# Sending tokens to their experts and back by products with a 0/1 matrix instead of through DRAM

## The chip, the cores and the metric

The kernel runs on one core of one Trainium2 chip. The metric is the device time of one execution in microseconds. Before the change it is 827.94 us, the median of three runs (826.21 to 828.65). The profile is of one more execution, and TensorE is PE in it, VectorE DVE, ScalarE ACT, GpSimd POOL, SyncE SP.

## The reference

One layer of a decoder for 256 prompt tokens and 8 sample tokens, all in fp32 with a width of 1024. Two attention mixers (a sparse one with 64 or 256 kept keys, and a stick-breaking one) are mixed by gates and projected; then comes a mixture of experts. Only its end is touched here:

```python
h = x + mixed @ w_out                      # 264 tokens x 1024
t = rmsnorm(h) * ln2_g
g  = top 1 of 4 groups (softmax of t @ w_rg + b);  e1, e2 = top 2 of the 8 experts in that group
combine[token, expert] = the two normalised expert weights times the group's weight, else 0
for every expert of 32:                    # w_gate, w_up: 1024 x 256, w_down: 256 x 1024
    hid = silu(t @ w_gate[e]) * (t @ w_up[e])
    y  += (hid * combine[:, e]) @ w_down[e]
out = rmsnorm(h + y) * ln_f_g
```

The three weight matrices of an expert are 1 MB each, 96 MB in all (100.66 million bytes), and all of them are read.

## The kernel before

Tokens are held in three tiles of rows (128, 128 and 8 tokens, `TILES`). Each expert has room for `CAP` = 32 tokens, and four experts form a quad of 128 slots. There are eight quads (`NQ`), and up to four more (`NQX` = 12), in branches, for tokens over 32 of one expert.

Routing. VectorE chooses experts from the router's logits (L1789 to L1821) and, from a rank that TensorE counts, gives each token two row numbers, one for each of its experts (L1830 to L1855): the row of a slot in a table of all slots. GpSimd scatters the tokens' numbers by these addresses to `table_dram` (L566) and loads the table to SBUF (L570). ScalarE has stored the normalised rows in `x2_dram` (L1374). Per quad GpSimd gathers 128 rows of `x2_dram` into `xg` (L577), TensorE transposes them (`turn`, L1099), ScalarE copies them to `xgT` (L1383).

Experts. `two_experts` (L1069) takes a pair of the quad at a time: 16 fp32 matmuls for gate and up (L1076; stationary 128x32 tokens, moving 128x512 weights; each expert writes its own 32 partitions), silu on ScalarE (L1390), the product on VectorE (L1877), two transposes, a copy, 8 matmuls for down (L1094). Every fp32 matmul is two records in the profile. ScalarE copies the result of a quad and stores it in `y_dram` (L1401), whose overflow part SyncE filled with zeros far ahead (L422).

Return. When the last store has landed, GpSimd gathers for each of the three tiles the first and the second expert's row (L592), and VectorE adds them with their weights to the residual `x_rows` (L1891, L1893). Then come the sum of squares (L1416), the mean (L1896), the power on GpSimd (L594), the scaling (L1899) and the stores of the output.

Weights. Four slots in `arena` hold one quad's weights. SyncE's queue is first in, first out, and all weights go through it. The first four experts are loaded ahead, during the output projection. Then, in a loop, gate and up of a pair are refilled when that pair's gate and up product is done (`s_gu`, L482), and down when its down product is done (`s_down`, L485). The order of work on each engine is written out by hand, and every engine takes its instructions in order. Ahead of all this SyncE waits at L436 for GpSimd's memset of `zero_i` (L557), which stands behind GpSimd's last gather of the attention caches, and only then issues w_proj_a and w_proj_b (L455, L456), for which TensorE waits at L1012.

## Time and profile before

| | |
|---|---|
| median of three runs | 827.94 us |
| the profiled execution's own time | 832.18 us |
| its span, first to last instruction | 830.3 us |
| busy: PE, PEld, DVE, ACT, POOL | 629.7, 356.3, 314.2, 149.9, 129.1 us |
| moved by DMA | 245.12 MB, mean 295 GB/s |
| mean granted TensorE clock | 0.864 |

The span covers all but 1.9 us of the execution's own time. A busy share is an average over stages with different limits; the slices and windows tell which engine is busy in which stage. [...] The DMA share is the mean busy share of 16 DMA engines and can come out a little over 1.

### The profile page before, as it was taken

What the parts mean: (1) busy time and instruction counts of PE and PEld (TensorE: products, weight loads), DVE (VectorE), ACT (ScalarE), POOL (GpSimd) and SP (SyncE); (2) the same over time, 40 slices, a digit from 0 to 9 for tenths busy, and PEclk for the clock granted to TensorE, in tenths of its full rate; (3) what the DMA queues carried; (4) which work ended last, traced back from release to release, by engine and by line L of the source; (5) the groups of instructions that cost most, each with busy time, mean ns of one, the idle gap of its engine ahead of it and who ended that gap; (6) DMA issues with size and microseconds to landing.
All of it is one profiled execution on the core that took longest, in us unless ns stands there. A gap on an engine that the chain in (4) does not pass through costs nothing.

```text
span 830.3 us, 7873 instructions
## 1 busy us (share of the span) xinstructions
PE 629.7 (76%) x3108; PEld 356.3 (43%) x3108; DVE 314.2 (38%) x490; ACT 149.9 (18%) x282; POOL 129.1 (16%) x119
## 2 busy tenths in 40 slices
PE   4969898997997898766899861586777877778710
PEld 3856764676885455325774251121222222222200
DVE  3079998987899870320230155000000000000005
ACT  2124033324104515330000100110110101101101
POOL 2434222111115352111000003100000000000020
PEclk9998899999999796987799955598998899989965
DMA  9997899588657889577789010199999999999631
GB/s 339 413 411 275 313 382 409 198 322 325 242 193 262 318 294 402 204 293 298 273 325 396 34 52 0 52 350 396 399 398 402 400 394 398 400 403 398 261 128 57
DMA packets 123916, 245.12 MB, mean 295 GB/s; under 512 B 14163, under 2 KB 86371, under 8 KB 113612
## 3 DMA queue, kind: packets, MB, share of 16 engines
q1 hardware_dynamic: 103932, 140.33, 46.0%
q0 software_dynamic: 14832, 94.98, 29.7%
q10 hardware_dynamic: 5120, 9.37, 3.1%
q8 instruction: 22, 0.36, 0.2%
q14 instruction: 10, 0.08, 0.0%
HBM read 232.66 MB, written 12.00 MB: 295 GB/s over the span
## 4 chain that ended last, share of the span: by engine, by line
PE 36%; SPq 23%; DVE 16%; DMA 9%; ACT 6%; issue 6%; POOL 2%; ACTq 1%; POOLq 0%; DVEq 0%
SPq L443 19%; PE PS L603 8%; PE PS L1030 5%; SPq L446 4%; DVE arena L1473 4%; PE PS L1021 4%; DVE x_rows L1477 4%; PE PS L1076 4%; PE PS L947 2%; DMA arena<-in_w_proj_b 2%; PE PS L1094 2%; DMA temp<-in_cache_k_a,page_idx 2%; PE PS L724 2%; DMA arena<-in_w_up 1%; PE PS L883 1%
## 5 line engine op out<-in xcount | busy, mean ns | idle before, releaser
L1076 PE MATMUL PS<-arena,temp 128*32 128x512 f32 x512 | 138.1, 701 | 37.4 <-DMA arena<-in_w_up 36.0
L603 PE MATMUL PS<-xT,arena 128*128 128x264 f32 x608 | 142.7, 394 | 4.6 <-ACT arena L1271 4.2
L603 PEld LDWEIGHTS PS<-xT,arena 128*128 128x128 f32 x608 | 116.2, 194 | 26.1 <-ACT arena L1271 4.8
L1877 DVE TENSOR_TENSOR temp<-PS,temp 64x256 f32<-64x256 f32 x16 | 6.8, 422 | 266.5 <-ACT temp L1390 266.5
L1076 PEld LDWEIGHTS PS<-arena,temp 128*32 128x32 f32 x512 | 39.5, 125 | 132.4 <-issue 132.4
L1473 DVE TENSOR_TENSOR arena<-arena,x_rows 128x2048 f32<-128x2048 f32 x32 | 73.0, 2283 | 28.8 <-DMA x_rows<-q_dram 28.7
L1477 DVE TENSOR_REDUCE x_rows<-arena 128x32 f32<-128x2048 f32 x32 | 73.2, 2288 | 1.1
L1094 PE MATMUL PS<-arena,temp 128*32 128x512 f32 x256 | 58.0, 594 | 12.3 <-ACT temp L1394 12.3
L503 POOL DMA_INDIRECT arena<-in_cache_k_b,unit_idx x32 | 39.5, 1234 | 147.5 <-DVE x_rows L1477 142.5
L503 POOL DMA_INDIRECT arena<-in_cache_v_b,unit_idx x32 | 37.6, 1176 | 78.4 <-PE PS L947 57.8
L503 POOL DMA_INDIRECT temp<-x_dram,slot_tok x9 | 8.6, 958 | 225.2 <-PE PS L1103 223.7
L1030 PE MATMUL PS<-temp,xT 128*128 128x512 f32 (+1 forms) x96 | 41.5, 593 | 1.1 <-DVE xT L1760 1.1
L1390 ACT ACTIVATE temp<-PS 64x256 f32<-64x256 f32 x16 | 6.1, 378 | 192.3 <-PE PS L1076 192.3
L1094 PEld LDWEIGHTS PS<-arena,temp 128*32 128x32 f32 x256 | 15.0, 109 | 44.4 <-issue 34.6
L1103 PE MATMUL PS<-consts,temp 128*128 128x128 f32 x72 | 11.2, 303 | 23.7 <-DMA temp<-x_dram,slot_tok 23.7
L1030 PEld LDWEIGHTS PS<-temp,xT 128*128 128x128 f32 (+1 forms) x96 | 14.9, 157 | 27.2 <-issue 27.2
L1138 ACT COPY arena<-PS 128x264 f32<-128x264 f32 x22 | 8.3, 379 | 85.7 <-PE PS L603 85.7
L1103 PEld LDWEIGHTS PS<-consts,temp 128*128 128x128 f32 x72 | 9.3, 197 | 30.5 <-issue 30.5
L1194 ACT COPY temp<-PS 128x512 f32<-128x512 f32 x32 | 17.5, 588 | 24.6 <-PE PS L724 24.6
L1021 PE MATMUL PS<-oaT,arena 128*128 128x264 f32 x64 | 17.5, 421 | 3.0 <-DMA arena<-in_w_proj_b 3.0
L947 PE MATMUL PS<-arena,xT 128*32 128x512 f32 x128 | 18.9, 705 | 0.0
L1767 DVE TENSOR_TENSOR x_rows<-PS,x_rows 128x512 f32<-128x512 f32 (+1 forms) x6 | 4.1, 687 | 38.3 <-PE PS L1030 38.3
(319 smaller groups left out, 722.1 us busy)
## 6 DMA issues: line engine op xcount, KB each, us to landing
arena<-in_w_gate SPq DMA_DIRECT2D x32, 1024.0 KB, 11.6
arena<-in_w_up SPq DMA_DIRECT2D x32, 1024.0 KB, 12.0
arena<-in_w_down SPq DMA_DIRECT2D x32, 1024.0 KB, 11.2
arena<-in_w_in SPq DMA_DIRECT2D x9, 2048.0 KB, 11.3
temp<-in_w_out SPq DMA_DIRECT2D x1, 4096.0 KB, 15.3
y_dram<-temp ACTq DMA_DIRECT2D x8, 512.0 KB, 6.5
x_rows<-in_x_prompt SPq DMA_DIRECT2D x2, 1024.0 KB
bias_dram<-x_rows SPq DMA_DIRECT2D x1, 2048.0 KB, 18.0
```

The costliest lines, as they stand in the source:

```text
L443: sp.dma_start(both[:, :, g, :], w[e].rearrange("o (p c) f -> (o p) c f", p=P)).then_inc(s_we[k], 16)
L446: sp.dma_start(slots[k][:, 16 * DE:24 * DE].rearrange("p (c d) -> p c d", c=2), we_down[e].rearrange("o (c p) d -> (o p) c d", p=P)).then_ ...
L503: pool.indirect_dma_start(out=dst, out_offset=None, in_=src, in_offset=bass.IndirectOffsetOnAxis(ap=idx, axis=0)).then_inc(landed, 16)
L603: last = nc.tensor.matmul(PS[0:m, n % 2, 0:T], w[:, k, c0:c0 + m], xT[:, k, :], start=(k == 0), stop=(k == KC - 1))
L947: last = nc.tensor.matmul(PS[r * 32:(r + 1) * 32, 0, :], a_pad[q][:, b % 4, 4 * u + r, :], v_slot(k)[:, r, :], start=(k % 16 == 0), stop=( ...
L1021: last = nc.tensor.matmul(PS[:, bank + c % 2, 0:T], w[:, k, c * P:(c + 1) * P], o[:, k, :], start=(k == 0), stop=(k == 3))
L1030: last = nc.tensor.matmul(PS[0:m, (ACC + 2 * t + n) % 8, :], mixT[:, k, t0:t0 + m], w_o[:, k, n * 512:(n + 1) * 512], start=(k == 0), stop ...
L1076: last = nc.tensor.matmul(PS[k * CAP:(k + 1) * CAP, 2 + n, :], xgT[:, d, k * CAP:(k + 1) * CAP], slots[k][:, d * 2 * DE:(d + 1) * 2 * DE], ...
L1094: last = nc.tensor.matmul(PS[k * CAP:(k + 1) * CAP, ACC + half, :], hidT[:, f, k % 2 * CAP:(k % 2 + 1) * CAP], slots[k][:, w0:w0 + 512], s ...
L1103: last = nc.tensor.transpose(PS[:, c // 4, c % 4 * QUAD:(c % 4 + 1) * QUAD], xg[:, c:D:KC], ident)
L1473: nc.vector.tensor_tensor(k_ring[:, u], k_ring[:, u], q_all[:, b % 2:b % 2 + 1, :].to_broadcast([P, 4, H * HD]), ALU.mult).then_inc(s_mul, 1)
L1477: nc.vector.tensor_reduce(z_s[:, b, :].rearrange("p (h r) -> p r h", r=R)[:, 4 * u:4 * u + 4, :], k_ring[:, u].rearrange("p r (h d) -> p r ...
```

## The change

No row goes through DRAM between routing and output. For each quad VectorE compares the tokens' row numbers, lowered by 128 per quad (`quad_row`), with 0..127 (`iota_slot`) and so writes two 0/1 matrices of 128 tokens by 128 slots per tile: `into`, and `back`, which holds the expert weights in place of ones. TensorE collects a quad's rows by six products with `into` stationary and the normalised rows moving (`collect`). The results of a quad are added to `x_rows` by six products with the transposed `back` stationary (`combine`) and six adds on VectorE (`add`); they run inside the next quad, and for the last one after the loop.

All four experts of a quad are taken at once (`gate_up`), in two halves of four chunks each; SyncE refills the halves of all four experts apart, each by DMAs of half the former size. The four quads of overflow remain in branches. The zero fill, the scatter, the table, the gathers and the stores of rows are gone, and so are SyncE's wait for `s_zero` and GpSimd's part in the loop. The last norm goes tile by tile. The silu, the hidden product and hid's copy take 128 partitions at once. The constant `zeros` gives its place to `iota_slot`.

Sums and products that only change names or semaphores are left out of the diff.

```diff
@@ sync
-            sp.dma_start(y_dram[NE * CAP:QUAD * NQX, :].rearrange("(p j) (k n) -> p (j k) n", p=P, n=P),
-                         const("zeros").unsqueeze(1).to_broadcast(...)).then_inc(s_yout, 16)
...
-            sp.dma_start(tok_i[:, :], a["token_ids"]).then_inc(s_tokid, 16)
-            sp.wait_ge(s_zero, 1)
-            sp.dma_start(table_dram.rearrange("(p t) o -> p (t o)", p=QUAD), zero_i[:, :]).then_inc(s_tokz, 16)
-            def gate_up(e, k):
+            def gate_up(e, k, half):
                 both = slots[k][:, 0:16 * DE].rearrange("p (c g f) -> p c g f", c=KC, g=2)
+                chunks = slice(half * 4, half * 4 + 4)
                 for g, w in enumerate((we_gate, we_up)):
-                    sp.dma_start(both[:, :, g, :], w[e].rearrange("o (p c) f -> (o p) c f", p=P)).then_inc(s_we[k], 16)
+                    sp.dma_start(both[:, chunks, g, :], w[e].rearrange("o (p c) f -> (o p) c f", p=P)[:, chunks, :]
+                                 ).then_inc(s_we[half], 16)
...
             with sp.Fori(1, NQ) as i:
-                for n in range(2):
-                    sp.wait_ge(s_gu, i * 2 + (n - 1))
-                    for k in (2 * n, 2 * n + 1):
-                        gate_up(bass.ds(i * 4 + k, 1), k)
-                    sp.wait_ge(s_down, i * 2 + (n - 1))
-                    for k in (2 * n, 2 * n + 1):
-                        down(bass.ds(i * 4 + k, 1), k)
+                sp.wait_ge(s_half, i)
+                for k in range(4):
+                    gate_up(bass.ds(i * 4 + k, 1), k, 0)
+                sp.wait_ge(s_gu, i)
+                for k in range(4):
+                    gate_up(bass.ds(i * 4 + k, 1), k, 1)
+                sp.wait_ge(s_down, i * 2)
+                for k in range(4):
+                    down(bass.ds(i * 4 + k, 1), k)
@@ tensor
+            def collect(i):
+                pe.wait_ge(s_into, i + 1)
+                for half in range(2):
+                    for t, (_, n) in enumerate(TILES):
+                        last = nc.tensor.matmul(PS[:, half, :], into[0:n, t, :], x2_rows[0:n, t, half * 512:(half + 1) * 512],
+                                                start=(t == 0), stop=(t == 2))
+                    last.then_inc(s_xg, 1)
...
+            def gate_up(half):
+                for d in range(4 * half, 4 * half + 4):
+                    for k in range(4):
+                        last = nc.tensor.matmul(PS[k * CAP:(k + 1) * CAP, 2, :], xgT[:, d, k * CAP:(k + 1) * CAP],
                                                 slots[k][:, d * 2 * DE:(d + 1) * 2 * DE],
                                                 start=(d == 0), stop=(d == KC - 1))
+            def combine(j):
+                t, half = j // 2, j % 2
+                t0, n = TILES[t]
+                return nc.tensor.matmul(PS[0:n, ACC + 2 + half, :], backT[:, t0:t0 + n], y_sb[:, half, :],
+                                        start=True, stop=True)
+            def quad(i):
+                pe.wait_ge(s_gT, i + 1)
+                pe.wait_ge(s_we[0], i * 128 + 128)
+                gate_up(0).then_inc(s_half, 1)
+                if not isinstance(i, int) or i:
+                    for j in range(6):
+                        if j >= 2:
+                            pe.wait_ge(s_add, i * 6 + (j - 7))
+                        combine(j).then_inc(s_comb, 1)
+                pe.wait_ge(s_back, i + 1)
+                for t, (t0, n) in enumerate(TILES):
+                    last = nc.tensor.transpose(PS[:, 3, t0:t0 + n], back[0:n, t, :], ident[0:n, 0:n])
+                last.then_inc(s_bt, 1)
+                more = not isinstance(i, int) or i < NQX - 1
+                if more:
+                    collect(i + 1)
+                pe.wait_ge(s_we[1], i * 128 + 128)
+                gate_up(1).then_inc(s_gu, 1)
+                if more:
                     turn(i + 1)
+                pe.wait_ge(s_hid, i + 1)
...
+                pe.wait_ge(s_wd, i * 64 + 64)
...
+                pe.wait_ge(s_btc, i + 1)
+                pe.wait_ge(s_y0, i + 1)
+                pe.wait_ge(s_y1, i + 1)
+                if not isinstance(i, int) or i:
+                    pe.wait_ge(s_add, i * 6)
+            for j in range(6):
+                if j >= 2:
+                    pe.wait_ge(s_fadd, j - 1)
+                combine(j).then_inc(s_fcomb, 1)
@@ scalar
+                act.wait_ge(s_bt, i + 1)
+                nc.scalar.copy(backT, PS[:, 3, 0:T]).then_inc(s_btc, 1)
+                if more:
+                    collected(i + 1)                    # xg[:, 0, :] from PSUM
+                act.wait_ge(s_gu, i + 1)
+                nc.scalar.activation(act_e, PS[:, 2, 0:DE], ACT.Silu).then_inc(s_act, 1)
+                if more:
+                    turned(i + 1)                       # xgT from PSUM
+                act.wait_ge(s_hT, i + 1)
+                nc.scalar.copy(hidT, PS[:, 2, 0:2 * P].rearrange("p (f m) -> p f m", f=2)).then_inc(s_hTc, 1)
+                act.wait_ge(s_down, i * 2 + 1)
+                nc.scalar.copy(y_sb[:, 0, :], PS[:, ACC, :]).then_inc(s_y0, 1)
@@ vector
+            def slots_in(i):
+                for t, (_, n) in enumerate(TILES):
+                    nc.vector.tensor_scalar(into[0:n, t, :], const("iota_slot")[0:n, :], quad_row[0:n, 0, t:t + 1],
+                                            None, ALU.is_equal).then_inc(s_step, 1)
+                dve.wait_ge(s_step, i * STEPS + 4)
+                for t, (_, n) in enumerate(TILES):
+                    last = nc.vector.scalar_tensor_tensor(
+                        out=into[0:n, t, :], in0=const("iota_slot")[0:n, :], scalar=quad_row[0:n, 1, t:t + 1],
+                        in1=into[0:n, t, :], op0=ALU.is_equal, op1=ALU.add)
+                last.then_inc(s_into, 1)
+            def slots_back(i):                          # 3 x 2 tensor_scalar (is_equal, mult), then 3 adds
...
+            slots_in(0)
...
+            slots_back(0)
+            collected(0)
...
+            def quad(i):
+                more = not isinstance(i, int) or i < NQX - 1
+                if more:
+                    nc.vector.tensor_scalar(quad_row[:, :, :], quad_row[:, :, :], -float(QUAD), None, ALU.add
+                                            ).then_inc(s_step, 1)
+                    dve.wait_ge(s_step, i * STEPS + (STEPS + 1))
+                    slots_in(i + 1)
+                if not isinstance(i, int) or i:
+                    for j in range(6):
+                        dve.wait_ge(s_comb, i * 6 + (j - 5))
+                        add(j, s_add)                   # x_rows += PS[:, ACC + 2 + half, :]
+                if more:
+                    dve.wait_ge(s_bt, i + 1)
+                    slots_back(i + 1)
+                    collected(i + 1)                    # xg[:, 1, :] from PSUM
+                dve.wait_ge(s_act, i + 1)
+                nc.vector.tensor_tensor(hid, PS[:, 2, DE:2 * DE], act_e, ALU.mult).then_inc(s_hid, 1)
+                dve.wait_ge(s_down, i * 2 + 2)
+                nc.vector.tensor_copy(y_sb[:, 1, :], PS[:, ACC + 1, :]).then_inc(s_y1, 1)
```

## Rows read from the trace of the kernel before

**Rows 1.** Page, the span in 40 slices of 20.8 us: granted clock, GB/s.

```profile
PEclk9998899999999796987799955598998899989965
GB/s 339 413 411 275 313 382 409 198 322 325 242 193 262 318 294 402 204 293 298 273 325 396 34 52 0 52 350 396 399 398 402 400 394 398 400 403 398 261 128 57
```

**Rows 2.** DMA issues: destination and source, queue, count, size, us to landing.

```profile
arena<-in_w_gate SPq DMA_DIRECT2D x32, 1024.0 KB, 11.6
...
y_dram<-temp ACTq DMA_DIRECT2D x8, 512.0 KB, 6.5
...
y_dram<-consts SPq DMA_DIRECT2D x1, 2048.0 KB, 37.4
...
temp<-x_dram,slot_tok POOLq DMA_INDIRECT x9, 7.4
```

**Rows 3.** Windows: stretch, length, busy of five engines, clock, DMA share, GB/s.

```profile
374.00:378.00 4.00, 3.83 (x112) 3.79 (x116) 0.00 (x0) 0.45 (x3) 1.14 (x2) 1.00 0.02 4
...
600.00:616.00 16.00, 12.88 (x53) 4.19 (x54) 0.04 (x1) 0.44 (x2) 0.00 (x0) 0.89 1.07 397
616.00:625.00 9.00, 5.66 (x28) 1.81 (x28) 0.38 (x1) 2.19 (x3) 0.94 (x1) 0.96 1.07 402
...
777.00:784.00 7.00, 6.30 (x22) 2.02 (x24) 0.00 (x0) 0.00 (x0) 0.00 (x0) 0.76 0.67 274
```

**Rows 4.** Timeline of SyncE: start, us, what it issues.

```profile
539.97 0.57 SPq L443 DMA_DIRECT2D arena<-in_w_gate  x1
...
568.63 0.57 SPq L443 DMA_DIRECT2D arena<-in_w_gate  x1
...
739.35 0.55 SPq L443 DMA_DIRECT2D arena<-in_w_gate  x1
```

**Rows 5.** Timeline of all engines around the first product.

```profile
509.36 0.17 DVE L1851 CAST row_i<-arena 128x6 int32<-128x6 f32 x1
...
522.24 1.02 POOL L503 DMA_INDIRECT temp<-x_dram,slot_tok  x1 [1.53 <-DMA slot_tok<-table_dram]
...
526.65 1.95 PE L1103 MATMUL PS<-consts,temp 128*128 128x128 f32 x8 [23.74 <-DMA temp<-x_dram,slot_tok]
...
529.95 9.83 PE L1076 MATMUL PS<-arena,temp 128*32 128x512 f32 x32 [1.35 <-ACT temp L1383]
```

**Rows 6.** Groups by line: count, busy us, mean ns, idle before.

```profile
L1030 PE MATMUL PS<-temp,xT 128*128 128x512 f32 (+1 forms) x96 | 41.5, 593 | 1.1 <-DVE xT L1760 1.1
...
L1767 DVE TENSOR_TENSOR x_rows<-PS,x_rows 128x512 f32<-128x512 f32 x4 | 2.8, 691 | 25.8 <-PE PS L1030 25.8
...
L1849 DVE TENSOR_TENSOR arena<-arena 128x96 f32<-128x96 f32 x2 | 0.5, 258 | 0.1
```

**Rows 7.** Timeline of TensorE in the last quad.

```profile
777.70 8.76 PE L1076 MATMUL PS<-arena,temp 128*32 128x512 f32 x32 [2.81 <-DMA arena<-in_w_up]
...
786.39 1.16 PE L1103 MATMUL PS<-consts,temp 128*128 128x128 f32 x8
...
788.82 3.63 PE L1094 MATMUL PS<-arena,temp 128*32 128x512 f32 x16 [0.99 <-ACT temp L1394]
```

**Rows 8.** Timeline of TensorE in the sample attention's value products.

```profile
306.68 3.64 PE L947 MATMUL PS<-arena,xT 128*32 128x512 f32 x32
```

**Rows 9.** Chain that ended last, in order of time: start, us, what.

```profile
382.37 19.01 DMA arena<-in_w_proj_b
...
793.80 4.37 DMA y_dram<-temp
```

**Rows 10.** Timeline of the return and the last norm.

```profile
800.33 0.95 POOL L503 DMA_INDIRECT arena<-y_dram,row_i  x1 [45.76 <-issue]
...
817.35 1.27 DVE L1893 SCALAR_TENSOR_TENSOR x_rows<-arena,x_rows 8x1024 f32<-8x1024 f32 x1
...
821.01 3.67 DVE L1899 SCALAR_TENSOR_TENSOR arena<-x_rows,small,temp 128x1024 f32<-128x1024 f32 x3 [1.01 <-POOL small L594]
```

**Rows 11.** Waits of TensorE from 95 to 270: us in total, times, longest.

```profile
PE PS L724 <- DMA arena<-in_cache_k_a,page_idx: 2.5, 1, 2.5
```

256 lines of the change are left out of this document (109 added, 147 removed).

## The prediction

> **What bounds the kernel now.** I read four views in turn. The page's slices show the last third of the span as one stage: from slice 28 on DMA moves some 400 GB/s, and not far before it lie four slices with at most 52, three of them at a granted clock of 0.5 [rows 1]. The DMA issues say what the traffic is: 96 loads of 1 MB of expert weights (gate stands for up and down, 32 each), and beside them eight 512 KB stores of y_dram and nine gathers of x_dram rows [rows 2]. The windows show that the DMA engines are full: share 1.07 at 397 GB/s while the weights run alone, 1.07 at 402 while a gather and a store run beside them [rows 3]. So in the loop every byte on any queue costs time. SyncE starts one turn of the loop at 568.63 and the fifth after it at 739.35 [rows 4]: 34.14 us for four experts, 12.58 MB of weights and 1.05 MB of gather and store, 13.63 MB at 399 GB/s. This traffic can't begin before the first gate-and-up product frees a slot, at 539.97 [rows 4]. The end is thus the sum of three pieces: the time until that first product, the bytes, and the tail after the last load.
>
> **The first product.** Now: the last step common to both kernels starts at 509.36 and ends at 509.53; then come address arithmetic, six scatters on GpSimd, a table load, the first gather from 522.24, its transposes at 526.65, a copy, and the product at 529.95, which takes 9.83 us for two experts [rows 5]. The change takes out scatter, table and gather. It adds on VectorE six 128x128 operations (slots_in); 128x96 takes 258 ns [rows 6], so about 0.3 us each, 1.8 together: 511.4. The weight arithmetic (L1824 to L1828) and nine more such operations (slots_back) are queued behind them and lie beside TensorE. Then collect(0): six fp32 matmuls, each two records; 96 records of the output projection took 41.5 us [rows 6], so 0.43 a record and 5.1 us for the twelve at full clock. The clock is at half (slices 24 to 26, rows 1). The 32 records at 529.95 take 9.83 us, while two experts side by side at full clock need 16 x 0.427 = 6.83: 3.0 us are lost before the clock is back. So collect(0) takes 8.1 (ends 5.1 and 10.2): 519.5. VectorE's copy of the second 128x512 half is like the add from PSUM, 0.69 [rows 6] (ScalarE's half lies beside matmuls); eight transposes are 1.16 when warm [rows 7]; from the transposes' end to the product stand 1.35 us now (528.60 to 529.95, rows 5): 522.7.
>
> gate_up(0) is four experts by four chunks, 32 records. What four column groups do side by side shows in the value products of the sample attention, with the same shapes (128x32 stationary, 128x512 moving): 32 records in 3.64 us [rows 8]. So 3.4 us, and the refill starts at 526.1 instead of 539.97: **14 us**. If the clock stays at half all through, 7.7.
>
> Does DMA then keep running? The first refill is 4.19 MB, 10.6 us. The second needs gate_up(1): after three transposes (0.45) and collect(1) (5.1), for which VectorE has slots ready about 526 (the overflow list stands before them), it ends near 535.1, before the first refill is through. The down refill follows at 541, while the second lasts to 548. No hole.
>
> **The bytes.** 7 stores and 7 gathers fall away between the first refill and the last load: 12.58 MB at 397 GB/s are 31.7 us a turn for 34.14, 2.44 x 7 = **17 us**. Against it, gate and up come as twice as many loads of half the size, 20 issues a turn for 12. SyncE's shortest issue is some 0.56 us [rows 4], 20 are 11 us, so issue doesn't bind. The pieces in the slot stay 1 KB. I take nothing for the split, with 0 and 0.3 us per added DMA as ends, up to 17 us; 0 is nearer, since the 12 loads of a turn follow each other with the engines full. [...]
>
> **What TensorE does in a turn,** since it gains work. At full clock: gate and up 2 x 3.42, combine 6 x 0.853 = 5.1, transposes of back 0.45, collect 5.1, from the end of gate_up to the down product 2.4 as now (786.46 to 788.82, rows 7; turn, silu and both copies lie in it) and 0.1 for the wider copy, down 3.42, the y copies 0.8: 24.3 us. After an idle of some 3 us the clock is at half: the product at 777.70 takes 8.76 for 6.83 [rows 7]. With 1.9 for that, 26.2 in 31.7. VectorE has 16 small operations at 0.3, six adds at 0.69 [rows 6] and 2 us of copies and product, some 11 us, and its add is shorter than a combine. So slots come free in time: the first half's slot 3.4 us after it has landed, while DMA has 8.4 MB (21 us) of other loads to do. The loop stays DMA's.
>
> **The tail.** Now DMA ends near 781.4 (0.67 of 1.07 of the window from 777 [rows 3]), 48.9 us before the end. After: 781.4 - 14 - 17 = 750.4. The last quad's first half has landed 21.1 us before, at 729.3, and TensorE needs 26.2 from there: 755.5, so TensorE is last, not the load. Leaving the loop: the store lands at 798.17 [rows 9] and GpSimd's first gather stands at 800.33 [rows 10], so 2.2 us for its branches; TensorE skips four longer bodies, not shown; ends 1.5 and 8, I take 3, near the row. Six combines, two at half clock, 6.8: 765.3. The add 0.9; then as now from the last sum's end (818.62) to the first scaling (821.01) 2.4, one scaling 1.3, and from the last VectorE end (824.68) to 830.3 5.6 [rows 10]: 775.5. The tail is 25.1, **23.8 us** less.
>
> **Two edits far ahead.** The 2 MB zero fill of y_dram (37.4 us to land, rows 2) leaves a stretch in which TensorE waits for cache_k_a 2.5 us in one piece [rows 11]: 0 and 3 are the ends, I take 1; TensorE's own order of work is late next. And SyncE no longer waits for GpSimd's memset before it issues w_proj. That load is now on the chain from 382.37 for 19.01 us [rows 9]. What can be gained is the idle DMA of 374 to 378, share 0.02 [rows 3]: 4 at most. But the last cache_v_a gathers, which TensorE needs first, then share DMA with the weights ahead of them; if they land later, all is given back. Ends -2 and +4, I take 0.
>
> **Sum.** 14 + 17 + 23.8 + 1 = 55.8 us. The span goes from 830.3 to 774.5, the profiled execution's own time from 832.18 to 776.4. That execution was 4.2 above the median of the runs shown, 827.94, which gives 772.1. I say 773.
>
> **The rivals.**
> (1) In this loop four column groups run at the pair's rate. Gate, up and down then take 20.5 for 10.3 and TensorE's turn is 34.6 with no idle: it bounds, 2.9 x 7 = 20 more in the loop and 7 in first product and tail: 800. For it: the present loop never shows more than two at once. Against: same shapes in rows 8. Chance 0.07.
> (2) The halved loads cost DMA 5 to 17 us, or the loop exit and a cold clock take their upper ends (5 and 6): 780 to 795. For it: the queue has not been run so, and the clock is at half ahead of the first product. Against: pieces unchanged, engines full now. Chance 0.23.
> (3) It gets slower: TensorE in the denser loop is granted half the clock for most of a turn, as it is after 777.70 for the first 4 us. Its 22 us of matmul become 44, a turn 46 and the whole near 915. It decides for slower once a turn is over 31.7 + 55.8/7.5 = 39.1 us: two thirds of the matmuls at half clock. Against it: 0.89 and 0.96 in windows of the loop [rows 3]. Chance 0.04.
> (4) The change doesn't do what it says, because overflow quads run and bring their own loads. Eight stores of y_dram [rows 2] are eight quads, so none runs with this routing. 0.01, at 805 (one more turn).
> The forecast has the remaining 0.65, own range 763 to 783. More is gained if w_proj pays 4 and the zero fill 3, or if the clock rises at once.
>
> **How the numbers follow.** The range goes from 763 to 796 and takes in (2); (1), (3), (4) and the far side are what is left out. A difference under 0.3% (2.5 us) can't be told from none. Only (3), and mishaps that I don't see, end at 828 or above: faster 0.94, same 0.01, slower 0.05.
>
> **What would show it.** Right: the first refill issued near 526; turns of 31.7 us at 397 GB/s; 32 records of gate_up in 3.4 us when warm; the last combine near 765; the w_proj loads issued near 374. Wrong: DMA share clearly under 1 in the loop with TensorE never idle (rivals 1 and 3, told apart by the granted clock); turns over 32.5 us with the share at 1.07 (rival 2); over 4 us between the last y copy and the first of the last combines.

## The result, and the profile after

The changed kernel takes **796.57 us** (median of four runs, 792.72 to 800.23) against 828.3 for the kernel before (four runs, 826.21 to 829.1): ratio 0.962, interval 0.957 to 0.967. Measured a second time, beside the experiments, it took 792.5 (six runs, 787.98 to 797.84) against 828.06: ratio 0.957, interval 0.952 to 0.962. The forecast was 773, its own range 763 to 783. So the change is faster, as forecast, but by 32 to 36 us in place of 55. Two executions of the experiments below, 845.69 us of e4 and 787.7 us of e10, fell into a slower state of the chip and are left out of their medians and ratios.

The profiled execution took 795.39 us, with a span of 793.6. First the page's slices, now of 19.8 us each (granted clock, GB/s), which answer to [rows 1]:

```profile
PEclk9998799999999678889579995599989989999886
GB/s 337 411 377 311 334 325 332 280 242 359 273 259 137 313 340 406 289 275 264 317 354 165 385 52 0 1 107 378 396 403 385 403 398 390 403 391 397 389 5 55
```

The stage at some 400 GB/s is still there: eleven slices of 378 to 403, now of 19.8 us, where before eleven of 20.8 (350 to 403) also held the stores and gathers. What stands out is the end: the last two slices move 5 and 55 GB/s, at a clock of 0.8 and 0.6. The kernel before had a long end too, but there data went out and came back.

SyncE's timeline answers to [rows 4] (start, us, what it issues): the first loads of a quad's first half.

```profile
527.08 0.39 SPq L435 DMA_DIRECT2D arena<-in_w_gate  x1
...
551.70 0.37 SPq L435 DMA_DIRECT2D arena<-in_w_gate  x1
...
710.56 0.37 SPq L435 DMA_DIRECT2D arena<-in_w_gate  x1
```

The refill starts at 527.08, against 539.97 before and 526.1 forecast. From 551.70 five turns lead to 710.56, 31.77 us each, against 34.14 before and 31.7 forecast. The DMA issues (destination and source, queue, count, size, us to landing) show the halved loads of [rows 2], and the windows (stretch, length, busy of five engines, clock, DMA share, GB/s) the loop and its end as in [rows 3]:

```profile
arena<-in_w_gate SPq DMA_DIRECT2D x64, 512.0 KB, 7.6
```

```profile
600.00:616.00 16.00, 11.81 (x69) 3.16 (x62) 4.40 (x12) 0.59 (x1) 0.00 (x0) 0.89 1.09 386
616.00:625.00 9.00, 9.00 (x27) 2.67 (x29) 4.94 (x13) 0.96 (x2) 0.00 (x0) 1.00 1.03 421
...
750.00:755.00 5.00, 5.00 (x30) 1.48 (x32) 0.69 (x1) 0.20 (x1) 0.00 (x0) 1.00 0.67 273
...
763.00:766.00 3.00, 0.00 (x0) 0.00 (x0) 0.05 (x1) 0.00 (x0) 0.00 (x0) 1.00 0.02 5
766.00:769.00 3.00, 0.00 (x0) 0.00 (x0) 0.00 (x0) 0.00 (x0) 0.00 (x0) 0.69 0.03 5
769.00:775.00 6.00, 0.40 (x1) 0.40 (x2) 0.00 (x0) 0.00 (x0) 0.00 (x0) 0.50 0.01 3
```

DMA is as full as before, with halved loads too, and by its share its work ends at about 753.3 (0.67 in the window from 750, where a full one has 1.02). That is the reckoning by which the forecast put it at 781.4 before; what waits for the last load sees it some 2 us later, as e6 and e10 will show. Then, from 763.06 to 774.60, no engine does anything: the row of 766:769 is empty but for 5 GB/s on DMA (e12 will show what moves), and the 0.40 us of TensorE in the last row are those from 774.60 on. The chain that ended last says the same in its own words (start, us, what); it is the view to read when all engines are idle:

```profile
762.36 0.70 DVE temp L1927
763.06 11.54 issue
774.60 8.58 PE PS L1063 x12
```

The last y copy ends at 763.06, and the first of the last combines starts 11.54 us later. "issue" is time for which the profile shows no releaser: here TensorE reads the count of overflow experts and passes the four `If` bodies that it doesn't enter. Before, that gap was not on the path of TensorE at all. I had said that over 4 us there would prove me wrong.

The rest of the early part (TensorE's timeline) answers to [rows 5] and [rows 8]:

```profile
510.68 7.86 PE L1039 MATMUL PS<-temp 128*128 128x512 f32 x12 [8.20 <-DVE temp L1856]
...
521.64 5.17 PE L1055 MATMUL PS<-arena,temp 128*32 128x512 f32 x32 [1.10 <-ACT temp L1385]
```

collect(0) takes 7.86 (forecast 8.1), gate_up(0) 5.17 for 3.4: the granted clock was 0.50 from 510 to 514, came up (0.95 from 514 to 519) and, behind two idle times of 1 us, went down again (0.74 from 519 to 524). In the loop, 32 records of gate_up and 32 of down take 3.64 us each, as in [rows 8].

### The profile page after: what moved, and what is told of

Its sections match the earlier page's. It is cut to its first block, busy times and chain, and to the rows that moved or that the text cites. A ratio compares the mean times of both kernels' runs of the same rounds, so it can differ in the third digit from the quotient of the medians.

```text
span 793.6 us, 8623 instructions
## 1 busy us (share of the span) xinstructions
PE 643.4 (81%) x3320; PEld 359.1 (45%) x3320; DVE 381.7 (48%) x682; ACT 150.7 (19%) x283; POOL 108.8 (14%) x98
## 4 chain that ended last, share of the span: by engine, by line
PE 42%; SPq 22%; DVE 16%; DMA 7%; ACT 5%; issue 5%; ACTq 1%; POOL 1%; DVEq 0%
SPq L435 20%; PE PS L568 9%; PE PS L995 5%; DVE arena L1474 4%; PE PS L986 4%; DVE x_rows L1478 4%; PE PS L912 3%; PE PS L1039 2%; SPq L439 2%; PE PS L1055 2%; DMA arena<-in_cache_v_a,page_idx 2%; PE PS L1063 2%; PE PS L689 2%; DMA temp<-in_cache_k_a,page_idx 1%; PE PS L1018 1%
## 5 line engine op out<-in xcount | busy, mean ns | idle before, releaser
L568 PE MATMUL PS<-xT,arena 128*128 128x264 f32 x608 | 147.5, 404 | 3.5 <-ACT arena L1273 3.2
L568 PEld LDWEIGHTS PS<-xT,arena 128*128 128x128 f32 x608 | 119.5, 199 | 26.6 <-ACT arena L1273 3.7
L1055 PE MATMUL PS<-arena,temp 128*32 128x512 f32 x512 | 72.5, 717 | 29.4 <-DMA arena<-in_w_up 27.0
L1905 DVE TENSOR_TENSOR x_rows<-PS,x_rows 128x512 f32<-128x512 f32 (+1 forms) x48 | 33.0, 688 | 81.7 <-PE PS L1063 81.7
L1039 PE MATMUL PS<-temp 128*128 128x512 f32 (+1 forms) x108 | 55.9, 644 | 8.2 <-DVE temp L1856 8.2
L1063 PE MATMUL PS<-temp 128*128 128x512 f32 (+1 forms) x96 | 48.5, 644 | 12.3 <-issue 12.3
L1055 PEld LDWEIGHTS PS<-arena,temp 128*32 128x32 f32 x512 | 17.3, 127 | 81.9 <-issue 46.0
L558 POOL TENSOR_TENSOR small<-small,consts 128x1 f32<-128x1 f32 x3 | 2.6, 876 | 305.9 <-DVE small L1945 305.9
L1098 PE MATMUL PS<-arena,temp 128*32 128x512 f32 x256 | 29.1, 595 | 9.1 <-ACT temp L1399 9.1
L1039 PEld LDWEIGHTS PS<-temp 128*128 128x128 f32 (+1 forms) x108 | 18.0, 192 | 38.9 <-issue 30.4
L1063 PEld LDWEIGHTS PS<-temp 128*128 128x128 f32 (+1 forms) x96 | 12.9, 165 | 48.0 <-issue 25.0
L1391 ACT COPY temp<-PS 128x264 f32<-128x264 f32 x8 | 3.0, 379 | 121.8 <-PE PS L1078 121.8
L1927 DVE COPY temp<-PS 128x512 f32<-128x512 f32 x8 | 5.5, 692 | 42.6 <-PE PS L1098 42.6
L1768 DVE TENSOR_TENSOR x_rows<-PS,x_rows 128x512 f32<-128x512 f32 (+1 forms) x6 | 4.1, 688 | 38.3 <-PE PS L995 38.3
L1876 DVE COPY temp<-PS 128x512 f32<-128x512 f32 x9 | 6.2, 692 | 32.9 <-PE PS L1039 32.9
## 6 DMA issues: line engine op xcount, KB each, us to landing
arena<-in_w_down SPq DMA_DIRECT2D x32, 1024.0 KB, 10.4
```

The source lines that it names most:

```text
L568: last = nc.tensor.matmul(PS[0:m, n % 2, 0:T], w[:, k, c0:c0 + m], xT[:, k, :], start=(k == 0), stop=(k == KC - 1))
L1039: last = nc.tensor.matmul(PS[:, half, :], into[0:n, t, :], x2_rows[0:n, t, half * 512:(half + 1) * 512], start=(t == 0), stop=(t == 2))
L1055: last = nc.tensor.matmul(PS[k * CAP:(k + 1) * CAP, 2, :], xgT[:, d, k * CAP:(k + 1) * CAP], slots[k][:, d * 2 * DE:(d + 1) * 2 * DE], sta ...
L1063: return nc.tensor.matmul(PS[0:n, ACC + 2 + half, :], backT[:, t0:t0 + n], y_sb[:, half, :], start=True, stop=True)
L1098: last = nc.tensor.matmul(PS[k * CAP:(k + 1) * CAP, ACC + half, :], hidT[:, f, k * CAP:(k + 1) * CAP], slots[k][:, w0:w0 + 512], start=(f ...
L1905: nc.vector.tensor_tensor(x_rows[0:n, t, cols], PS[0:n, ACC + 2 + half, :], x_rows[0:n, t, cols], ALU.add).then_inc(added, 1)
```

## The experiments

Every kernel ran beside the kernel before, whose median over these runs was 827.5 to 829.8. The early part of the program differs by up to 8 us from one execution to the next: the projection starts at 401.15 in "after", and between 394.6 and 402.9 in the runs with the same code up to there. So each profile is also read in stages: from the projection's first product to the first refill, and from the refill to the end of the span. In us:

| kernel | span | projection | first refill | between | refill to end |
|---|---|---|---|---|---|
| before | 830.3 | 401.4 | 540.0 | 138.6 | 290.3 |
| after | 793.6 | 401.2 | 527.1 | 125.9 | 266.5 |
| after, again | 786.3 | 395.4 | 521.5 | 126.1 | 264.8 |
| e1_no_overflow | 775.1 | 396.2 | 522.4 | 126.2 | 252.7 |
| e2_nested | 779.5 | 395.9 | 522.1 | 126.3 | 257.4 |
| e3_bytes_back | 805.2 | 394.6 | 521.0 | 126.4 | 284.2 |
| e4_late_refill | 839.0 | 401.2 | 537.6 | 136.3 | 301.4 |
| e6_lean_end | 779.3 | 395.0 | 521.4 | 126.4 | 257.9 |
| e7_wproj_b_behind | 786.6 | 392.0 | 523.0 | 131.0 | 263.6 |
| e8_warm | 790.3 | 400.8 | 523.7 | 122.9 | 266.6 |
| e9_before_no_overflow | 823.4 | 398.2 | 536.8 | 138.6 | 286.6 |
| e10_count_early | 779.4 | 401.7 | 528.2 | 126.4 | 251.2 |
| e11_best | 768.0 | 391.9 | 515.5 | 123.6 | 252.5 |
| e12_short_bodies | 783.6 | 402.9 | 529.2 | 126.3 | 254.4 |

### Is the gap the overflow branches? (e1, e2)

e1 takes the count and the branches out of every engine:

```diff
-            n_extra = pe.value_load(ovf_i[0:1, 0:1], min_val=0, max_val=NOVF)
-            for t in range(NQ, NQX):
-                with pe.If(n_extra > 4 * (t - NQ)):
-                    quad(t)
```

> The kernel after, without the overflow quads, their branches and the read of their count on SyncE, TensorE, ScalarE and VectorE (with this routing none of them runs, but a routing that needs them would lose tokens). Theory A, the skipped branches cost the time: between the last y copy (763.06 in the kernel after) and the first of the last combines (774.60) 11.5 us shrink to under 2, and the span goes from 793.6 to about 782, some 1.5 of it because the combines find the clock less cold. Rival B, it is the loop's exit or something that every kernel of this form pays: the gap stays over 8 us and the span above 790. Rival C, the wait is for another engine (y copy, adds) that the trace puts down wrongly: the gap stays, and the span too.

Measured: 780.67 us (776.91 to 785.3), ratio 0.942, interval 0.935 to 0.948. Its chain at the same place:

```profile
758.52 0.47 issue
758.99 5.71 PE PS L1054 x12
```

The 11.54 us are 0.47, and the combines take 5.71 for 8.58, since TensorE's clock did not fall (granted 1.00 from 745 to 765). Refill to end falls by 13.8 (266.5 to 252.7): 11.1 from the gap, 2.9 from the combines. The count and its branches are the cause. This kernel leaves the loop at the same place, so the loop's end is in the 0.47 too, and rival B fell.

e2 keeps them, but puts each body inside the one ahead (on TensorE, ScalarE and VectorE), so that a run without overflow passes one branch and not four:

```diff
-            for t in range(NQ, NQX):
-                with pe.If(n_extra > 4 * (t - NQ)):
-                    quad(t)
+            def overflow(t):
+                with pe.If(n_extra > 4 * (t - NQ)):
+                    quad(t)
+                    if t + 1 < NQX:
+                        overflow(t + 1)
+            overflow(NQ)
```

> The kernel after, with the four overflow branches nested on TensorE, ScalarE and VectorE, so that a run without overflow jumps once instead of four times; the code that is jumped over is the same. Theory A1, each taken jump costs about 11.5/4 = 2.9 us: the gap is 3 to 4.5 us and the span about 785. Rival A2, the length of the code jumped over costs, however often one jumps: the gap stays at 10 to 12 us, span 793. Rival B, the loop's exit: the same as A2 here, told apart by the run without branches.

Measured: 784.0 (781.36 to 791.83), ratio 0.947, interval 0.940 to 0.954. The chain:

```profile
756.34 5.12 issue
761.46 7.60 PE PS L1063 x12
```

The 5.12 us are a little over A1's 3 to 4.5 and far from A2's 10 to 12. Three branches fewer are 11.54 - 5.12 = 6.42 us, 2.14 each. With 0.47 for the plain release there remain 5.12 - 0.47 - 2.14 = 2.5 for the read of the count. With these, 0.47 + 2.5 + 4 x 2.14 = 11.5. This takes the first branch for as dear as the others; e12, below, corrects it.

### Was it hidden before? (e9)

My 3 us came from the kernel before, where 2.2 us lie between the store's landing and GpSimd's first gather. e9 is the kernel before without the overflow branches:

> The kernel before, with the overflow branches left out on every engine (no expert overflows with these inputs, so the output is the same). The question is why the exit of the loop was not seen in the trace before, where I took 3 us from. Theory A (hidden there): before, the end of the last pair goes to DRAM and is gathered back, and the engines read the count and jump while that transfer is under way, so leaving them out gains at most 2 us: ratio 0.997 to 1.0, 826 to 829. Theory B (it cost as much there, and I read the row wrongly): about 11 us are gained, as in the changed kernel, 816 to 819, ratio near 0.986.

Measured: 824.85 (ten runs, 820.97 to 829.86), ratio 0.995, interval 0.991 to 0.999. Refill to end is 3.7 shorter. Its chain and, behind it, the part of the chain of the kernel before that lies between [rows 9] and [rows 10]:

```profile
790.77 2.58 DMA y_dram<-temp
793.35 0.26 issue
793.61 0.94 POOL arena L494
```

```profile
798.19 0.49 POOLq L583
...
798.99 0.05 POOLq L585
...
799.47 0.04 POOLq L585
```

GpSimd reads the count (L583) and passes its four comparisons (L585, the first at 798.99 and the last at 799.47) 0.16 us apart: 2.2 us from the landing at 798.17 to the gather at 800.33 for all of it, where TensorE pays 2.14 for one branch. TensorE, VectorE and ScalarE passed theirs too before, and no step of the chain waited for them; what the trace shows of TensorE's stands under e12. So the cost was there and hidden: theory A, though 3.8 us were gained and not its 2 (1.9 from the branches of GpSimd, 1.8 since the store was seen sooner: 2.58 for 4.37). The row I took my 3 us from was of an engine whose bodies are a gather and a wait; TensorE's body is a whole quad, some 130 matmul records. That the length of the body is what makes a branch dear fits both rows; e12 puts it to the test.

### Does the length of the body make the branch dear? (e12)

e12 is the changed kernel with the same count and four branches on TensorE, over short bodies (its overflow quads are left out):

```diff
                 with pe.If(n_extra > 4 * (t - NQ)):
-                    quad(t)
+                    pe.wait_ge(s_into, t + 1)
+                    nc.tensor.matmul(PS[:, 3, :], ident, consts[:, 0:512], start=True, stop=True)
```

> The changed kernel with the same read of the count and the same four branches, one behind the other, but on TensorE the body of each is one wait and one 128x512 product in place of a whole quad of some 130 matmul records (so TensorE leaves out the overflow quads; none is entered with these inputs). The other engines are as in the changed kernel. Theory A (a branch is dear because it jumps over a long body, to code that the engine doesn't have at hand, as the rows of GpSimd suggest, 0.16 us a branch over short bodies): the gap between the last y copy and the first of the last combines falls from 11.5 us to between 2 and 4.5 (0.47 of release, 4 x 0.16 of branches, up to 2.5 for the read and the end of the loop), refill to end 256 to 259 against 264.8 and 266.5, time 784. Theory B (a branch costs TensorE 2.1 us whatever it jumps over): gap 11.5, time as the changed kernel, 792 to 797. [...]

Measured: 785.07 (782.72 to 787.58), ratio 0.948, interval 0.944 to 0.953. The chain:

```profile
763.32 2.43 issue
765.75 7.42 PE PS L1063 x12
```

11.54 us are 2.43. Less 0.47, the read of the count and all four short branches are 1.96 together. So theory A: of the gap in "after", 9.1 us come from the length of the bodies that TensorE jumps over, 2.3 a branch. It also corrects the split from e2: since the read is at most 1.96, e2's single branch costs at least 5.12 - 0.47 - 1.96 = 2.7.

What the 9.1 us are spent on can be read from the DMA queues (kind, packets, MB, share) in each gap alone: "after" from 763.06 to 774.60, e2 from 756.34 to 761.46, e12 from 763.32 to 765.75, and for comparison the kernel before from 790 to 800.33:

```profile
q8 instruction: 3, 0.05, 1.8%
...
q8 instruction: 1, 0.02, 1.6%
...
DMA packets 0, 0.00 MB, mean 0 GB/s; under 512 B 0, under 2 KB 0, under 8 KB 0
...
q8 instruction: 3, 0.05, 2.3%
```

Nothing moves in the gap of "after" but three packets of 16 KB on a queue that the profile calls instruction, near 765.4, 768.7 and 772.2; in e2's gap there is one, near 758.7, in e12's and e1's none. (One more stands behind each gap, near 775.5 and 762.1.) Only TensorE's program differs between e12 and "after", so the packets come with TensorE's long bodies. e2's gap is 2.69 us longer than e12's with one packet in it, that of "after" 6.42 longer than e2's with two more: 2.7 to 3.2 us for each packet. That describes the gaps better than a price per branch: four jumps have three packets in their gap, and e2's one jump past all four bodies has one. What a packet holds, and which engine waits for it, no trace shows; that TensorE waits for each is an estimate of mine from these lengths. The kernel before shows such packets near 791.1, 794.6, 798.2 and 801.2, 3.0 to 3.6 us apart as in "after" (3.3 to 3.5), beside its last products, the store and the gathers, and e9 none between 780 and 800: what goes with TensorE's jumps was there before too, and hidden.

### The changed kernel once more (e5)

> The kernel after, unchanged, as the measure for the three that run beside it, and to see how its time spreads (792.7 to 800.2 so far). The time from the first refill to the end should be 266.5 us within 2 again; what varies should lie ahead of it (it was 527.1 there, while two kernels that are the same up to that point had 522.1 and 522.4).

Measured: 792.5 (787.98 to 797.84), ratio 0.957, interval 0.952 to 0.962. The stage from refill to end agrees within 1.7 us with the first profile, and its gap ahead of the last combines is 11.17 us, again with three packets on the instruction queue; what differs is the early part, where the projection starts at 395.4 and not at 401.2. So between these two runs of one kernel lie some 6 us that no experiment explains, and the experiments are compared by their stages.

### The bytes (e3)

e3 puts 1.05 MB a turn back: ScalarE stores 512 KB to a scratch in DRAM and loads 512 KB from an input into rows that nothing reads.

```diff
+                act.dma_start(junk_dram[rows, :], gf_all).then_inc(s_js, 16)
+                act.wait_ge(s_jl, i * 16 + 16)
+                act.dma_start(g2_all, a["x_prompt"][0][0:P, :]).then_inc(s_jl, 16)
```

> The kernel after, with one 512 KB store to DRAM and one 512 KB load added per quad on ScalarE's queue, of rows that nobody uses; the output is unchanged. They are the bytes that stores and gathers had in the kernel before. Theory: every byte on any queue costs time in the loop, so a turn goes from 31.74 us back to 34.1 to 34.3 and the span grows by some 17 us, to 811. Rival: the turn of 34.14 before came from weights waiting for slots or from GpSimd's queue, and DMA has room for 1 MB more: turns stay under 32.3, span under 798.

Measured: 807.1 (807.03 to 810.54), ratio 0.973, interval 0.967 to 0.979. SyncE's first gate loads:

```profile
583.89 0.37 SPq L437 DMA_DIRECT2D arena<-in_w_gate  x1
...
720.83 0.37 SPq L437 DMA_DIRECT2D arena<-in_w_gate  x1
```

Four turns in 136.94 us, 34.24 each: the turn of the kernel before to within 0.1. Refill to end grows by 17.7 over "after" (19.4 over its second profile). The step "17 us for the bytes" stands, and the halved loads cost nothing that shows.

### The early refill (e4)

In e4 SyncE refills the first half only when both halves have been used:

```diff
-                sp.wait_ge(s_half, i)
+                sp.wait_ge(s_gu, i)
                 for k in range(4):
                     gate_up(bass.ds(i * 4 + k, 1), k, 0)
-                sp.wait_ge(s_gu, i)
```

> The kernel after, but SyncE refills both halves of gate and up only when the second half's product is done; the loads stay 512 KB. Theory: only the start moves, from 527.1 to some 537, because in the loop the first half is asked for about 2 us before DMA runs dry; turns stay at 31.7 to 32.2, the span grows by 10 to 13 us, to 803 to 807. Rival: the early half matters in every turn, since a refill that is asked for 2 us ahead leaves a hole: turns of 33 to 35 us and a span of 813 to 826.

Measured: 838.88 (nine runs, 831.75 to 840.84), ratio 1.009, interval 1.005 to 1.013. My expectation was a miss: not only the first refill comes later (10.4 us), every turn grows, from 31.7 to 37.7. The windows of one turn, in the columns from above, and TensorE's wait at its end:

```profile
610.00:615.00 5.00, 5.00 (x43) 2.11 (x42) 1.12 (x2) 0.53 (x2) 0.00 (x0) 1.00 0.23 94
615.00:620.00 5.00, 3.78 (x34) 0.97 (x32) 0.02 (x1) 1.73 (x3) 0.00 (x0) 1.00 0.92 292
620.00:625.00 5.00, 0.00 (x0) 0.00 (x0) 2.28 (x8) 0.00 (x0) 0.00 (x0) 0.93 1.01 302
```

```profile
629.89 2.79 PE L1054 MATMUL PS<-arena,temp 128*32 128x512 f32 x12 [9.98 <-DMA arena<-in_w_up]
```

From 610 to 615 DMA has almost nothing to do (0.23): all of its weights have landed, and no slot has come free (SyncE waits 13.6 us for TensorE's L1054 before it issues again at 613.97). That is 3.9 us of 5, and another 2.6 are lost at about 300 GB/s in the ten after it; together the 6 of the turn. In the changed kernel the half that was used first is refilled while the other half lands. With all four experts refilled at once the rest of the change gives nothing: this kernel is no faster than the one before, which had its pieces too (it refilled pair by pair) and a turn of 34.14. e4 also shows that "DMA is full" is a state that the order of the refills keeps up, not a property of the loop.

### The end, further (e6, e10)

e6 nests the branches as e2 does and leaves out, in the last quad, the collect and transposes of a quad that does not run (they move into the first overflow branch):

```diff
-                more = not isinstance(i, int) or i < NQX - 1
+                more = not isinstance(i, int) or i not in (NQ - 1, NQX - 1)
```

> The kernel after with its end made shorter: the last quad stands behind the loop and doesn't collect or turn rows of a ninth quad; the overflow quads are nested branches, and the first of them collects its own rows. Theory: the nested jump gives 6.4 us of the gap (11.5 to 5.1) and 1 of the combines; without collect (5.9) the last gate_up follows the back transposes when its half has landed, and the down product starts when the last load lands, near 753.3 instead of 758.7: 5 more. From first refill to end 266.5 - 12 = 254. Rival: the last load, not TensorE, sets the end already, and the peeled quad only adds code to fetch: 257 to 260.

Measured: 786.82 (781.1 to 791.4), ratio 0.950, interval 0.945 to 0.955: no better than e2. The rival was right (257.9 us from refill to end, in its 257 to 260). TensorE's timeline:

```profile
749.73 6.07 PE L1098 MATMUL PS<-arena,temp 128*32 128x512 f32 x32 [3.80 <-DMA arena<-in_w_down]
...
761.46 7.41 PE L1063 MATMUL PS<-temp 128*128 128x512 f32 x12 [5.65 <-issue]
```

TensorE was ready for the down products some 5 us sooner than in e2 (225.0 us after the first refill, for 229.8), was idle for 3.80 until the last weights had landed, and worked at a granted clock of 0.50 from 750 to 754 (0.83 to 756), so the down products took 6.07 for 3.64. Then the count and the branch again. The last weights are seen 17.1 us after the issue of w_down (732.61), in e10 16.3. In "after", with the issue at 738.37, that is 754.7 to 755.5, and the down products start at 758.66: there TensorE was last, by some 3 to 4 us.

e10 keeps e6's last quad, and lets the engines read the count ahead of the last wait for weights, and TensorE wait for the last y copies behind the branch:

```diff
+                if ahead:
+                    ahead()          # wait for s_ovf, value_load of the count
                 pe.wait_ge(s_wd, i * 64 + 64)
...
-                pe.wait_ge(s_btc, i + 1)
-                pe.wait_ge(s_y0, i + 1)
-                pe.wait_ge(s_y1, i + 1)
+                if not ahead:
+                    settle(i)        # these waits
...
             overflow(NQ)
+            settle(NQ - 1)
```

> The kernel with nested branches and a last quad without the next quad's collect (e6), and in it the count is read by each engine before the last wait for weights (TensorE waits 3.8 us there anyway), and TensorE's waits for the last y copies stand behind the jump, so that the jump can be taken while the down products run. Theory A (the read and the jump are work of the sequencer, which runs ahead of the queued products): the 4.9 us between the last y copy and the first combine fall to 0.5, refill to end 253.5 against 257.9, about 782.5. Theory B (the jump costs only once the queue is empty, because the code behind it is fetched then): the read is hidden but some 2.1 us are left, refill to end 255.8, about 784.7. Theory C (no gain, the engine that is late is VectorE or ScalarE, with their own reads): 257.9.

Measured: 779.38 (five runs, 775.92 to 781.25), ratio 0.940, interval 0.936 to 0.944. The chain:

```profile
763.05 0.24 issue
763.29 5.69 PE PS L1063 x12
```

0.24 us between the copy and the combine, less than in e1, and the branches are still there. Theory A: the branch is passed while the products ahead of it are being executed, so what takes e2 5.12 us behind a wait leaves 0.24 when it stands ahead of it; the packets stand at 756.8, 758.6 and 762.0, beside the down products (755.90 to 762.27). The combines, behind an idle of 1.02 us and not of e6's 5.65, run at a granted clock of 1.00 from 763 to 769 (5.69 us), where e6's had 0.50 from 761 to 763 and 0.84 to 769 (7.41 us), and refill to end is 251.2, 6.7 under e6 and 1.5 under e1.

### The early part (e7, e8)

e7 holds w_proj_b back until five of cache_v_a's products are done:

```diff
+            sp.wait_ge(s_vaused, 5)
             sp.dma_start(w_pb, a["w_proj_b"][0].rearrange("(k p) n -> p k n", p=P)).then_inc(s_wp, 16)
```

> The kernel after, with the second half of the projection weights (w_proj_b) issued only when the product of the fifth cache_v_a gather is done; w_proj_a stays early. Theory: what the earlier w_proj loads gave was lost because they took DMA from the cache_v_a gathers that TensorE waits for (1.9 to 7.2 us before each of four products). Then the last of these products starts near 387 instead of 393.6 and the first projection near 395 instead of 401.2, if w_proj_b has landed by then: 4 to 6 us less, measured from the last value product (369.5). Rival: DMA has to move the same bytes before the projection, w_proj_b lands last instead, and the projection starts at 400 to 402 as now.

Measured: 788.35 (783.56 to 791.11), ratio 0.951, interval 0.946 to 0.956. In "after" the w_proj loads are issued at 369.52, 12 us sooner than before (SyncE no longer waits for GpSimd), and the projection starts at the same 401. From the start of the block of 128 products to the projection it is 26.2 us before and 26.9 in e9, but 29.4 to 30.0 in the kernels with early w_proj loads: the early issue cost some 3 us there. TensorE's timeline says where that went, first "after", then e7:

```profile
371.17 3.70 PE L928 MATMUL PS<-arena,temp 128*32 128x128 f32 x128
382.03 1.94 PE L928 MATMUL PS<-arena,temp 128*32 128x128 f32 x32 [7.16 <-DMA arena<-in_cache_v_a,page_idx]
...
393.57 1.94 PE L928 MATMUL PS<-arena,temp 128*32 128x128 f32 x32 [1.99 <-DMA arena<-in_cache_v_a,page_idx]
...
401.15 2.10 PE L986 MATMUL PS<-oaT,arena 128*128 128x264 f32 x4 [0.93 <-issue]
```

```profile
366.98 3.70 PE L929 MATMUL PS<-arena,temp 128*32 128x128 f32 x128
...
385.23 1.08 PE L929 MATMUL PS<-arena,temp 128*32 128x128 f32 x32 [2.11 <-DMA arena<-in_cache_v_a,page_idx]
...
391.95 3.86 PE L987 MATMUL PS<-oaT,arena 128*128 128x264 f32 x8 [0.93 <-issue]
```

The four products wait for gathers that share DMA with the weights issued ahead of them (from issue to landing 12.0 us in "after", 9.9 in e7, 7.8 before, medians). From the block of 128 to the projection it is 30.0 us in "after" and 25.0 in e7: 5 gained. Of these, 2.9 are shorter waits (10.0 for 12.9 in four), and 2.1 faster products: the clock stayed at 0.50 in "after" from 382 to 396, and was 0.96 in e7 from 380 to 387. The profiled span shows nothing of it (786.6 us, 786.3 in e5) and the medians 4 us, since the stretch from projection to refill grew by 5. Two rows of e7's timeline say why:

```profile
502.25 11.49 PE L1040 MATMUL PS<-temp 128*128 128x512 f32 x12 [8.19 <-DVE temp L1857]
...
517.67 5.04 PE L1056 MATMUL PS<-arena,temp 128*32 128x512 f32 x32 [1.10 <-ACT temp L1386]
```

collect(0) took 11.49 at a granted clock of 0.50 (from 502 to 514), 7.86 in "after" where it rose on the way (0.50 to 514, then 0.95). The waits ahead are the same (8.19, 8.20). So the clock came back at another step in two runs of the same code.

e8 keeps TensorE at work through the waits of the router, with 21 products into a PSUM bank that nothing reads:

```diff
+            def warm_2(n):
+                for _ in range(n):
+                    nc.tensor.matmul(PS[:, 3, :], ident, consts[:, 0:512], start=True, stop=True)
+            warm_2(5)     # ahead of the second norm's transposes
...
+            warm_2(7)     # behind the router's product
...
+            warm_2(9)     # behind the ranks, ahead of collect(0)
```

> The kernel after, with 21 products of constants into an unused bank (5, 7 and 9, 0.85 us each) put into TensorE's three waits between the output projection and collect(0). Theory: TensorE then keeps the granted clock at 1.00 from 474 to 530; the router's product takes 4.5 to 7 instead of 8.1 us, collect(0) 5.2 to 6 instead of 7.9, gate_up(0) 3.6 instead of 5.2; from the output projection's end to the first refill 52.5 us become 45 to 48, and the end moves as much. Rival: the clock stays at half in spite of these products, or they delay what waits behind them, and nothing is gained (52 to 54 us).

Measured: 789.71 (788.5 to 799.79), ratio 0.955, interval 0.949 to 0.960. Windows of e8, columns as above, and its collect(0):

```profile
480.00:492.00 12.00, 10.04 (x65) 9.53 (x66) 4.84 (x8) 0.00 (x0) 0.00 (x0) 0.66 0.01 1
499.00:511.00 12.00, 11.72 (x41) 5.67 (x39) 8.83 (x43) 0.00 (x0) 0.00 (x0) 1.00 0.00 0
```

```profile
509.16 6.00 PE L1046 MATMUL PS<-temp 128*128 128x512 f32 x12 [0.28 <-DVE temp L1863]
```

collect(0) falls to 6.00 and projection to refill by 3.0; gate_up(0), behind 3 us of copies and transposes, still takes 5.16 (clock 0.50 from 518 to 520). The theory promised more: 4.5 to 7.5 us, a router product of 4.5 to 7 us (it took 8.02) and a clock of 1.00 throughout (0.66 from 480 to 492). By the total alone, 789.7 cannot be told from 792.5; the stage shows the 3 us.

### All of it (e11)

> All that helped, together: e10, w_proj_b issued behind five of cache_v_a's products (e7), extra products that keep TensorE's clock up before the router and the first quad (e8), and four extra products while TensorE waits for the last down weights. If the gains add: projection start 5 us earlier, projection to refill 123 instead of 126 (the 5 us that e7 lost again behind the output projection are a cold first quad: its collect took 11.5 us against 7.9, and the extra products should mend that), refill to end 264.8 less 4.3 less 7 less 2.5 = 251: about 770 against 792.5, ratio near 0.930. If they take each other's place (the last load of weights sets the end, wherever the rest goes): 776 to 780.

Measured: **770.19** (767.43 to 774.67), ratio 0.931, interval 0.927 to 0.935. It beats both kernels and all others here. The gains add: 770 was expected. Refill to end is 252.5 for 251. Its last steps on TensorE:

```profile
741.89 5.39 PE L1134 MATMUL PS<-consts 128*128 128x512 f32 x8 [1.30 <-ACT temp L1432]
747.21 3.64 PE L1116 MATMUL PS<-arena,temp 128*32 128x512 f32 x32
751.86 5.68 PE L1071 MATMUL PS<-temp 128*128 128x512 f32 x12 [1.01 <-DVE temp L1978]
```

Down and combines run at full clock (1.00 from 747 to 758). The four extra products are a little too many: in e10 and e6 the down products start 16.3 and 17.1 us after SyncE's w_down issue, here 19.6 (727.60 to 747.21), so the weights had landed some 3 us before 747.2. From refill to end it is no better than e10. Two extra products might do better; that was not tried.

## Why the prediction was wrong

By the first profile: forecast span 774.5, measured 793.6, 19.1 us missing. They are found at five places. The second profile of the same kernel (786.3) has the same gap and misses 11.8: its early part is 5.7 shorter, by a spread that the forecast had no term for.

- **Leaving the loop: forecast 3 us, ends 1.5 and 8; measured 11.54. This is the step that failed** (8.5 us, and past its upper end). The sentence was "2.2 us for its branches; TensorE skips four longer bodies, not shown". I had the right question, and bounded it by a row of another engine whose bodies are short. e1, e2 and e12 show what it consists of: 0.47 of release and loop's end, at most 2.0 for the read and four comparisons, and 9.1 or more for four jumps over long bodies, beside three packets of 16 KB on the instruction queue; e9 and the packets of the kernel before show that this was hidden there.
- **TensorE's last turn: 26.2 us forecast, 29.2 measured** (733.89 to 763.06), 3.0. gate_up(0) took 6.56 for 5.3, combines 5.71 for 5.1, collect 6.00 for 5.1, and 32 records 3.64 for 3.42. I priced a 128x512 record at 0.427 from two groups side by side and 0.43 from the output projection; in collect a record takes 0.50. A mis-sized term; the mechanism (TensorE ends last, not the load) held. e6 shows how near the load is: without the collect TensorE is idle until it lands.
- **The last load: 750.4 forecast, 753.3 measured**, 1.0 from the first refill and 1.9 in the loop. The last quad's first half landed 19.4 us ahead of it, not 21.1; that is because the end by share (753.3) lies before the landing that a wait sees (754.7 to 755.5), and the first half was timed by a wait. Together 4.6 on the path.
- **The last combines: 6.8 forecast, 8.6 measured,** which with the last add is 1.6 more (9.3 for 7.7), and 0.4 behind them: 2.0. That follows from the first point: TensorE had done nothing for 11 us and came back at a granted clock of 0.50, which rose only from 780 on (0.80 to 782, then 1.00); in e1 they took 5.71.
- **The zero fill and w_proj: 1 and 0 forecast, together 0 measured** (projection at 401.15 for 401.42). They can't be told apart. The block of 128 products starts 4.0 us sooner than before, but in e9, which keeps the zero fill, it starts 3.9 sooner too; behind it some 3 us go to the gathers of cache_v_a that share DMA with the early w_proj loads (e7), which is below the -2 that I gave as the lower end.

8.5 + 3.0 + 4.6 + 2.0 + 1.0 = 19.1.

What held: the first product (14 us; 12.9 measured); the turn (31.7 us; 31.8), e3 gives the 2.4 us back when the bytes come back; the halved loads at nothing; of w_proj the reason (the last gathers land later), though not the size; and no hole in DMA after the first refill. On that last point e4 shows that I had seen the halves as a matter of the first refill only: against refilling all four experts at once they are worth 6 us in every turn.

Of the rivals, (1) fell: four column groups run 32 records in 3.64 us, in the loop too. (3) fell: the loop's windows show 0.89 and 1.00. (Its 915 was also wrongly added up: a turn of 46 for 31.7, over the 7.5 turns that I used two sentences on, gives some 880.) (2) is what came true in one of its two parts, the upper end of exit and clock, and beyond it: I gave it 0.23 and 780 to 795, and the second measurement of the same kernel (792.5) lies in it. The range ended at 796 since I took 8 us as the most that the exit could cost. An unknown of which the trace of before shows nothing on the engine concerned deserved an end further out: four bodies, each of which could cost as much as GpSimd's whole passage (2.2), give 8.8, and the read comes on top.

## What to carry to other kernels

A body that isn't entered is not free: a jump over a long one cost TensorE 2.14 us and more, and four over short ones, with the read of the count, at most 1.96 together. Behind a wait the jumps stood on the path in full (11.54 us); ahead of the wait, with work queued on the engine, 0.24 us were left (e10). When a change takes a detour away, list what the other engines did during the detour: here leaving out count and branches gains 13.8 us behind the refill in the changed kernel and 3.7 in the one with the detour through DRAM, which hid the rest, and the forecast had counted the whole detour as gain. If engines are idle and nothing seems to hold them, look at what the instruction queue moves: here one packet for every 2.7 to 3.2 us of the gap.

What kept DMA full here while the weights streamed (396 GB/s) was that a piece came free while another landed: a turn took 31.77 us so, and 37.7 with all experts refilled at once (e4). Check each turn, not only the first, for the moment at which everything has landed and nothing is free. And price a step from a row of the same engine, the same shape and the same number of groups; where there is none, set the far end by what each repetition could cost.

## What the runs showed of the hardware

- On TensorE, an `If` around a quad of some 130 matmul records that is not entered takes 2.14 us and more, and in the gap stands one packet of 16 KB on the instruction queue for every 2.7 to 3.2 us; around one product, four of them with the read of the count take at most 1.96 together (e12); on GpSimd, one around a gather and a wait takes 0.16.
- 20 queued loads of 0.5 and 1 MB move 12.58 MB in 31.77 us, 396 GB/s, as fast as the kernel before moved its 13.63 MB a turn, 399 GB/s with 12 loads of 1 MB: no loss at half the size, with the queue kept full.
- TensorE's granted clock at the end of "after" was 1.00 until 766, 0.69 to 769 and then 0.50, and 0.50 still from 775 to 780, in full work, behind an idle of 12.30 us. The last six combines took 8.58 us, most of them at 0.50, and 5.71 at 1.00 (e1). Behind an idle of 1.0 to 1.2 us it was 1.00 at these combines in e1, e10 and e11, and with products in the place of idleness from 499 to 511 in e8.
- 32 fp32 records of 128x512 with four column groups take 3.64 us at a granted clock of 1.00, in the attention (from 306.68, before) as in the loop ("after", from 752.48).
